# The feed-forward up projection by Strassen's scheme, with f kept in DRAM until the down projection

## What is computed

```python
def conv_ffn(h, w_up, conv_w, conv_b, w_down):      # h: 1024 x 1024, D_FF = 2816
    s = h.shape[1]
    u = h @ w_up                                     # 1024 x 5632
    u_pad = jnp.pad(u, ((0, 0), (CONV_WIDTH_2 - 1, 0), (0, 0)))
    u = conv_b + conv_w[0] * u_pad[:, 0:s] + conv_w[1] * u_pad[:, 1:1 + s] + conv_w[2] * u_pad[:, 2:2 + s]
    gate = u[..., :D_FF]
    val = u[..., D_FF:]
    return (jax.nn.silu(gate) * val) @ w_down        # back to 1024 x 1024, added to x
```

## Time and profile before

| | us |
|---|---|
| median of 3 runs | 2482.22 (2477.52 to 2484.29) |
| profiled execution, its own time | 2483.62 |
| its span | 2482.0 |
| PE busy | 2451.3 (99%) |
| DVE busy | 1416.7 (57%) |
| ACT busy | 806.5 (32%) |
| POOL busy | 95.5 (4%) |

### The profile page before, as it was taken

How to read it: one execution, slowest core, us unless ns; L and a number is a source line. 1 busy time by engine, 2 the same in 40 slices (tenths; PEclk the granted TensorE clock), 3 DMA queues, 4 the chain that set the end, 5 groups by cost and what they waited for, 6 DMA issues and landing times.

```text
span 2482.0 us, 31910 instructions
## 1 busy us (share of the span) xinstructions
PE 2451.3 (99%) x11696; PEld 2036.9 (82%) x11696; DVE 1416.7 (57%) x2288; ACT 806.5 (32%) x1513; POOL 95.5 (4%) x112
## 2 busy tenths in 40 slices
PE   8999999999999999999999999999999999999998
PEld 6888888888888888887788888988888888888876
DVE  5747887787532243436455753553687257734775
ACT  5334544444521121321233352453232112211224
POOL 1000000000000000021000020012000000000000
PEclk9999999999999999999999999999999999999999
DMA  5111111111111131222110142451111111111123
GB/s 197 34 43 52 43 51 51 43 59 46 48 51 51 46 115 51 86 75 56 35 46 26 35 140 85 137 178 51 43 51 48 45 51 51 44 50 51 44 63 123
DMA packets 236403, 160.97 MB, mean 65 GB/s; under 512 B 5294, under 2 KB 223571, under 8 KB 235298
## 3 DMA queue, kind: packets, MB, share of 16 engines
q1 hardware_dynamic: 229456, 132.66, 18.0%
q0 software_dynamic: 4976, 18.75, 2.2%
q10 hardware_dynamic: 1890, 8.43, 1.0%
HBM read 138.85 MB, written 20.97 MB: 64 GB/s over the span
## 4 chain that ended last, share of the span: by engine, by line
PE 96%; DVE 2%; DMA 1%; ACT 1%; issue 0%; SPq 0%; ACTq 0%; DVEq 0%
PE bank L717 26%; PE bank L718 26%; PE bank L719 26%; PE bank L1051 1%; PE bank L872 1%; PE bank L1052 1%; PE bank L1053 1%; PE bank L1248 1%; PE bank L1250 1%; PE bank L1249 1%; PE bank L1104 1%; PE bank L1103 1%; PE bank L1105 1%; DMA wraw<-in_w_in_dram 1%; PE bank L883 1%; PE bank L884 1%
## 5 line engine op out<-in xcount | busy, mean ns | idle before, releaser
L717 PE MATMUL bank<-xhi,whi 128*128 128x512 f32 x1056 | 411.8, 390 | 0.6 <-DVE wlo L1860 0.6
L719 PE MATMUL bank<-xhi,wlo 128*128 128x512 f32 x1056 | 410.9, 389 | 0.0
L718 PE MATMUL bank<-xlo,whi 128*128 128x512 f32 x1056 | 410.9, 389 | 0.0
L1860 DVE TENSOR_TENSOR wlo<-wraw,whi 128x1024 fp32r<-128x1024 f32 (+1 forms) x240 | 285.3, 1189 | 151.4 <-ACT whi L1282 101.6
L1289 ACT ACTIVATE whi<-wraw 128x1024 fp32r<-128x1024 f32 x132 | 139.5, 1057 | 573.9 <-PE bank L719 569.1
L717 PE MATMUL bank<-x4hi,whi 128*128 128x512 f32 x704 | 274.3, 390 | 0.0
L719 PE MATMUL bank<-x4hi,wlo 128*128 128x512 f32 x704 | 273.9, 389 | 0.0
L718 PE MATMUL bank<-x4lo,whi 128*128 128x512 f32 x704 | 273.9, 389 | 0.0
L717 PEld LDWEIGHTS bank<-xhi,whi 128*128 128x128 f32 x1056 | 198.2, 188 | 42.5 <-DVE wlo L1860 0.7
L718 PEld LDWEIGHTS bank<-xlo,whi 128*128 128x128 f32 x1056 | 198.2, 188 | 41.5 <-issue 0.2
L719 PEld LDWEIGHTS bank<-xhi,wlo 128*128 128x128 f32 x1056 | 198.2, 188 | 41.3
(11 more groups left out here) (397 smaller groups left out, 4515.2 us busy)
## 6 DMA issues: line engine op xcount, KB each, us to landing
wraw<-in_w_in_dram SPq DMA_DIRECT2D x85, 512.0 KB, 3.9
wraw<-in_ffn_w_up_dram SPq DMA_DIRECT2D x44, 512.0 KB, 3.8
wraw<-in_xattn_wkv_dram SPq DMA_DIRECT2D x16, 512.0 KB, 4.0
wraw<-in_ffn_w_down_dram SPq DMA_DIRECT2D x16, 512.0 KB, 4.0
wraw<-in_ffn_w_down_dram SPq DMA_DIRECT2D x16, 384.0 KB, 3.5
xraw<-in_x_dram SPq DMA_DIRECT2D x4, 1024.0 KB, 10.1
x_spill<-xt SPq DMA_DIRECT2D x8, 512.0 KB, 2.8
conv_spill<-tv POOLq DMA_DIRECT2D x8, 512.0 KB, 3.1
```

Source lines behind the costliest of these rows:

```text
L717: pe.matmul(acc, whi[slot][:, k, :], xh, start=(k == 0), stop=False)
L718: pe.matmul(acc, whi[slot][:, k, :], xl, start=False, stop=False)
L719: last = pe.matmul(acc, wlo[slot][:, k, :], xh, start=False, stop=(k == k_tiles - 1))
L1860: dve.tensor_tensor(wlo[slot][:, 0:n, :], wraw[slot][:, 0:n, :], whi[slot][:, 0:n, :].bitcast(F32), ALU.subtract).then_inc(s_wlo, 1)
```

## The change

The 1024 x 1024 block of x and the 1024 x 256 block of weights of a pair are each seen as 2 by 2 blocks: the two halves of the tokens and the two halves of the 8 feature blocks for x, the same halves of the feature blocks and gate against value for the weights. Strassen's scheme in Winograd's form gives the four result blocks (gate and value for each half of the tokens) by seven products of half the depth instead of eight.

- The seven right-hand forms of x (`b11`, `b21`, `b22` as they are, `t1` to `t4` sums and differences) are made once, the first four behind the attention's output projection, the others during the first pair, by DVE (`form_sum`, `form_lo`) and ACT (`form_hi`). They take the place of `x4hi` and `x4lo`.
- The seven left-hand forms of each pair's weights (`a11`, `a12`, `a22`, `s1` to `s4`) are made for every pair: POOL makes the four sums (`weight_sum`), ACT seven high parts (`weight_hi`), DVE seven low parts (`weight_lo`), each of 128x512.
- PE's `form_product` is 4 blocks times 3 matmuls. Products 2, 3, 5 and 6 (counted from 0) add onto a bank that holds an earlier product, which must first have been copied out (`first_copy` on ACT) or added (`result` on DVE).
- The factor `R` is now multiplied in by POOL for three of the four quarters (`normed`), by DVE for one. ACT computes the first tap (`tap0`), DVE the other two (`taps`), POOL the product of silu and value (`product`).
- f is not split at once: `store_f` writes it to DRAM. The down projection comes after all 22 pairs; `load_f` brings f back, ACT and DVE split it (`f_hi`, `f_lo`, 128x1024 each), and three accumulations over 8, 8 and 6 blocks follow.

The diff, cut to its core:

```diff
+PRODUCTS = (("a11", "b11"), ("s2", "t2"), ("a12", "b21"), ("s3", "t3"), ("s1", "t1"), ("a22", "t4"), ("s4", "b22"))
...
+            def form_product(n, p, ready=None):
+                a, b = PRODUCTS[n]
+                o, onto = ps(FORM_BANKS[n]), n in (2, 3, 5, 6)
+                pe.wait_ge(s_alo, 7 * p + (lo_order.index(a) + 1))
+                for k in range(HK):
...
+                    pe.matmul(o, ahi[a][:, k, :], xh, start=(k == 0 and not onto), stop=False, skip_group_check=True)
+                    pe.matmul(o, ahi[a][:, k, :], xl, start=False, stop=False, skip_group_check=True)
+                    last = pe.matmul(o, alo[a][:, k, :], xh, start=False, stop=(k == HK - 1), skip_group_check=True)
+                last.then_inc(s_m, 1)
...
+                pe.wait_ge(s_p1, p + 1)
+                form_product(2, p, (lambda k: 3 * k + 5) if first else None)
...
+            def weight_sum(name, p):                    # GpSimd
+                if name == "s3":
+                    ins = pool.tensor_tensor(to, a11, a21, ALU.subtract)
+                if name == "s2":
+                    ins = pool.tensor_tensor(to, a22, araw["s3"][:, :, :], ALU.subtract)
+                if name == "s1":
+                    ins = pool.tensor_tensor(to, a21, a22, ALU.add)
+                if name == "s4":
+                    ins = pool.tensor_tensor(to, a12, araw["s2"][:, :, :], ALU.subtract)
...
+            def normed(p, u, h, n):
+                pool.wait_ge(s_c, 6 * p + n)
+                pool.tensor_tensor(u_h, u_h, R[:, h * HALF:(h + 1) * HALF], ALU.mult).then_inc(s_rm, 1)
+            def product(p, h):
+                pool.wait_ge(s_act, 2 * p + h + 1)
+                pool.wait_ge(s_tap, 4 * p + 2 + h)
+                pool.tensor_tensor(yv[:, half], yv[:, half], yg[:, half], ALU.mult).then_inc(s_prod, 1)
...
+            def first_copy(p):                          # ScalarE
+                act.wait_ge(s_m, 7 * p + 1)
+                    act.wait_ge(s_tap, 4 * p - 1)
+                act.activation(uv[:, 2:2 + HALF], ps(2 * G0), ACT.Copy).then_inc(s_p1, 1)
...
+            def weight_lo(name, p):                     # VectorE
+                if name in ("s2", "s3"):
+                    dve.wait_ge(s_as, 4 * p + (4 if name == "s2" else 2))
+                dve.tensor_tensor(alo[name][:, :, :], src, ahi[name][:, :, :].bitcast(F32), ALU.subtract)\
+                    .then_inc(s_alo, 1)
...
+            def f_lo(n):
+                dve.wait_ge(s_ffn_hi, n + 1)
+                dve.tensor_tensor(flo[n][:, :], fraw[n][:, :], fhi[n][:, :].bitcast(F32), ALU.subtract)\
+                    .then_inc(s_ffn_lo, 1)
```

More of the change, by code:

```diff
@@ L63 @@
 T_FF = T_XO + 8
-T_LAST = T_FF + sum(2 * n + 8 for n in FF_GROUPS) - 8
+T_LAST = T_FF + 16
 T_END = T_LAST + 16
@@ L318, in hybrid_then_mixer_kernel @@
         s_par2 = sem("later_params_loaded")
+        s_part = [sem(f"part_loaded{n}") for n in range(8)]
         s_x = [sem(f"x_loaded{n}") for n in range(4)]
@@ L1714, in _ @@
             x_q_hi(0, 0)
[L1715 removed]
+            act.wait_ge(s_pw_loaded, 32)
             for a in range(2):
@@ new lines, in _ @@
+            act.wait_ge(s_ms, 8)
+            act.activation(x4root[:, :], ps(6)[:, 0:NB], ACT.Sqrt, bias=eps[:, 0:1], scale=1.0 / D).then_inc(s_rs, 2)
+            late_hi(5)
+            form_term(7)
+            late_hi(6)
+            late_hi(7)
+            for h in range(2):
+                act.wait_ge(s_ms, 9 + h)
+                act.activation(R[:, h * HALF:(h + 1) * HALF], ps(6 + h), ACT.Copy).then_inc(s_r, 1)
+            for k in range(HK):
+                form_hi("b22", k, resid[:, HK + k, HALF:S], gain(HK + k))
@@ new lines, in _ @@
+            up_step(0, first=True)
+            with act.Fori(1, LASTP) as i:
+                up_step(i)
+            up_step(LASTP, last=True)
+            tap0(LASTP, uv, yv, 1, 3, FF_TILES)
+            f_hi(5)
+            tap0(LASTP, ug, yg, 1, 4, 0)
+            f_hi(6)
+            tanh(LASTP, 1)
+            f_hi(7)
+            act.wait_ge(s_m, 7 * FF_TILES)
+            for n in range(8, 12):
+                load_f(n)
+            for n in range(8):
+                split(T_FF + n + 2, (T_FF + n) % 2)
+                f_hi(8 + n)
+                if n == 0:
+                    act.wait_ge(s_fst, 16 * FF_TILES)
+                if n < 4:
+                    load_f(12 + n)
@@ new lines, in _ @@
+            late_lo(4)
+            late_sum(6)
+            late_lo(5)
+            result(2, 0)
+            late_sum(7)
+            late_lo(6)
+            late_lo(7)
+            weight_lo("a22", 0)
+            result(3, 0)
+            for k in range(HK):
+                form_lo(25 + k, "b22", k, HK + k, 1)
+            weight_lo("s4", 0)
+            result(4, 0)
+            dve.wait_ge(s_r, 8)
+            result(1, 0)
+            weight_lo("a11", 1)
+            weight_lo("a12", 1)
@@ new lines, in _ @@
+            taps(0, ug, yg, 0, 1, 0)
+            silu(0, 0)
+            weight_lo("s3", 1)
+            weight_lo("s2", 1)
+            weight_lo("s1", 1)
+            weight_lo("a22", 1)
+            with dve.Fori(1, LASTP) as i:
+                order.enter(i, 4, 1)
+                up_step(i)
+                order.leave(LASTP)
+            up_step(LASTP, last=True)
+            result(5, LASTP)
+            f_lo(4)
+            taps(LASTP, uv, yv, 0, 2, FF_TILES)
+            taps(LASTP, uv, yv, 1, 3, FF_TILES)
@@ new lines, in _ @@
+            f_lo(5)
+            taps(LASTP, ug, yg, 1, 4, 0)
+            f_lo(6)
+            silu(LASTP, 1)
+            f_lo(7)
+            for n in range(16):
+                t = T_FF + n
+                for h in range(2):
+                    dve.wait_ge(s_acc, 2 * t + h + 1)
+                    r = resid[:, n % KT, h * HALF:(h + 1) * HALF]
+                    dve.tensor_tensor(r, ps(2 * (t % 2) + h), r, ALU.add).then_inc(s_free, 1)
+                split(t + 2, t % 2)
+                if 8 + n < FF_TILES:
+                    f_lo(8 + n)
```

665 lines of the change are left out of this document (516 added, 149 removed).

## The result

The changed kernel takes 2554.97 us (median of 4 runs, 2551.22 to 2557.13), the kernel before 2482.41 (4 runs, 2477.52 to 2484.29): a ratio of 1.0289, with a 95% interval from 1.0276 to 1.0302. The forecast was 2554, in a range from 2478 to 2620. The mechanism was right.

What follows compares the result with a forecast made beforehand. PE was taken as the bound. First pair 20.0, second 7.5, others 20 x 1.6, squares -1.9, down tile 11.0, clock 3: 71 us on 2483.6 gave 2555, median 1.4 lower, so 2554; range 2478 to 2620.

Steps and rivals of the forecast that it cites:

- The bound before: In the feed-forward network PE alone is the bound: two waits, 1.3 us out of 718 us.
- the matmuls taken away: In the 22 pairs, 264 matmuls fewer, 59.9 us; 84 remain per pair, 19.05 us.
- The exclusion: In the pairs, POOL operations reading SBUF and DVE operations with two SBUF inputs exclude one another; together 22.1 us per pair.
- Rival one: No exclusion counts in the loop, PE bounds it at 19.05 us per pair: -26 us, 2456 us; chance 0.18.
- The fixed part read from the copies: Some 0.18 us of a POOL operation do not scale with columns, so one of 128x512 takes 1.29 us.
- The chain in the loop: From the end of product 5 to product 2, 12.2 us; PE waits 4 us, a pair takes 23.35.
- three operations of POOL come first (3.8 us): After product 5, value times R, the s4 sum and value times R precede DVE's low parts: 3.8 us.
- small waits: In each loop pair, short PE waits before products 5 and 6, about 0.3 us.
- The clock: Rival: the clock falls in every pair behind the product 2 wait, 2.7 us x 21 = 57 us, 2611; chance 0.13.
- The ends: First pair 41.8 us instead of 21.8, plus 3 for clock; second 29.2; PE waits 11.0 in the first down tile.
- the sums over squares: Behind the attention, two sums over squares now lie within the first pair: 1.9 us taken off.
- The rows to look for: Profile after: 84 matmuls in 23 to 24 us, longest PE wait at product 2, POOL operations 1.3 to 1.9, PE share 88%.

Runs made afterwards that it cites:

- section 2: Changed kernel with POOL's two-SBUF-input operations in the feed-forward part replaced by a tiny operation and eight memsets, so almost no reads: 2451.18 us, ratio 0.987.
- sections 1, 2 and 5: Section 1 and section 2 have their own lines; 5 is the changed kernel with DVE's second and third taps summing in PSUM: 2475.69 us.
- The own tile: Changed kernel with ACT's copy of product 0 put in a tile of its own: 2522.66 us.
- the other orders: Changed kernel with the own tile, copy and result 0 earlier in ACT's and DVE's queues, POOL's first sums ahead of the last sum of squares, no PSUM: 2524.01 us.
- the two moves on POOL: Changed kernel with gate-value products behind all taps, 2505.49 us; separately, with the fourth weight sum ahead of the second value half times R, 2510.46 us.
- the PSUM operands: Changed kernel with ACT's first tap written to PSUM and DVE's second and third taps using the running sum there: 2475.69 us, ratio 0.9968.
- the dose run: Changed kernel with only POOL's four weight sums per pair replaced by a tiny operation and eight memsets: 2489.8 us, a single run.
- the fastest kernel: Changed kernel with the other orders, taps through PSUM, and POOL's fourth weight sum moved ahead of value times R: 2460.95 us, 0.9921 of the kernel before.
- section 1: Separate kernel of only 128x512 operations, each engine alone, then two together: 16 on DVE beside 8 on POOL take 18.24 us, against 19.5 one after the other.

## Why the prediction was right, and where it was not

**The bound before and the matmuls taken away** were right: section 2 shows 19.04 us per pair where no read of POOL interferes.

**The exclusion** was right, including the inference that DVE is held when POOL is first; sections 1, 2 and 5 show it. Rival one, no exclusion in the loop, forecast 2456 us. That is near what the run without reads gives (2451, though that run leaves work of POOL out), with the loop at 19.04 us as the rival had it: its premise was false, and its sum stood up. The fixed part read from the copies gave 1.29 us for a POOL operation of 128x512; weight sums and unheld products show 1.29, the operations with R 1.09.

**The chain in the loop** was mis-sized: from the end of product 5 to product 2 I walked 12.2 us, and the trace has 10.95 (product 6 starts at 1997.03, product 2 at 2007.98). The step that failed is "three operations of POOL come first (3.8 us)". They take 3.4 (1996.99 to 2000.38), because two of the three are the 1.09 us form. The rest of the walk takes 7.6 us instead of 8.4, since low parts and taps overlap their hand-overs more than I allowed. The pause was thus 2.64 us, not 4, and small waits 0.5, not 0.3.

**The clock** was put into a rival with 0.13, on the ground that the pause might be too short or that products 0 and 1 stand before it. In fact it fell in every pair, at a pause even shorter than I assumed, and cost 1.71 us rather than 2.7. As terms of the loop, 19 pairs at +1.6 were 30 us and measured +2.12 each, 40.3. So the step that failed here is the term for the clock, put at nothing in the sum. Per pair the pause was 4.0 - 2.64 = 1.36 too much, the clock and the small waits 1.71 + 0.19 too little; 0.54 are left, 23.89 against 23.35. That they nearly cancel is luck.

**The ends** were over-priced. The first pair takes 39.3 us with its clock loss (forecast 41.8 + 3). Product 0 waits 1.58 us, not 3.2. Product 1 waits 7.71, not 8.8, and then takes 5.21 us, mostly at 1.2 GHz (2.5 us lost, 3 expected). From product 3 on 6.3 us are added, not 7.9. And the 41.8 themselves don't add up: 19.05, the waits of 3.2, 8.8 and 7.9 and the 1.9 of the sums over squares are 40.85, so 0.95 us have no term. The second pair is 27.75, not 29.2, and 2.4 of that are clock which the forecast did not have (its product 1 takes 5.1 us). The first down tile takes 20.68 us, 9.8 more than its 10.88 (forecast 11.0 of waits); 6.0 are waits, and most of the rest is low clock behind the longest of them (granted 0.50 and 0.51 in the 8 us from 2294). Together: 17.5 + 6.0 + 40.3 + 1.65 (last pair) - 1.9 + 9.8 = 73.35 us, against 20 + 3 + 7.5 + 30.4 + 1.6 - 1.9 + 11 = 71.6. The ends gave back 8 of the 10 us that the loop lacked, and nothing in the working made sure of that.

**The rows to look for** came as said, apart from two: PE's longest total wait at product 2 behind ACT's `ffn_u_value` (51.2 us), 84 matmuls in 23.89 us, DVE's taps up to 1.63, PSUM operations at 0.68. POOL's operations lie between 1.09 and 1.70, not 1.3 and 1.9. PE's share, too, was not as said: it was 96% of the span and 90% of the loop, not 88%, because a slow matmul counts as busy; the granted clock of 0.93 in the loop was the row to watch.

What stays open: how the 3.13 us of pauses divide between held time and order. The own tile, alone and with the other orders (22.11 and 22.20), shows that they move without shrinking; the two moves on POOL take 0.8 of them each; the PSUM operands take 2.3. These shares overlap, since a shorter hold also moves the next.

## To carry to other kernels

Before work goes to an idle GpSimd, list which of its operations and of VectorE's read SBUF, and add both lists as if they were one engine's; if the sum nears the bound engine's time, give VectorE's operations a PSUM operand where a bank is free, and order GpSimd's queue so that what others wait for isn't behind what waits itself. A pause of TensorE in a loop has two prices, its length and the low clock behind it: splitting or filling it can pay as much as removing it. The longest wait in the profile names one dependency, not the bound, and freeing it alone can move the wait.

## What the hardware showed that I had not expected

- Operations with one SBUF operand take part in the exclusion: DVE's tensor_scalar and POOL's copy (section 1). In the run without reads POOL's additions of 4 columns are shown with 0.2 to 0.66 us on average, by tile. A small read waits behind a long one as well: the one shown first below lasts until 1975.01, and DVE's tap beside it until 1974.96; where DVE is not in the way such an addition takes 0.20 us.

```profile
1974.38 0.63 POOL L777 TENSOR_TENSOR ffn_u_gate<-ident 128x4 f32<-128x4 f32 x1 [1.59 <-DVE ffn_u_gate L3068]
...
1974.22 0.74 DVE L3075 SCALAR_TENSOR_TENSOR ffn_value<-ffn_u_value,pcol,ffn_value 128x512 f32<-128x512 f32 x1
...
L777 POOL TENSOR_TENSOR ffn_u_gate<-ident 128x4 f32<-128x4 f32 x21 | 13.8, 658 | 32.7 <-DVE ffn_u_gate L3068 32.7
```

- PE's clock is sensitive to small differences of a pause that recurs: behind 2.48 us of waiting it was granted 0.57 in the next 4 us, behind 1.76, 1.61, 1.53 and 1.16 us (orders without PSUM, the two moves on POOL and the dose run) 1.00. A change that shortens the pause from the one to the other gains 1.7 us on top. The length of the wait alone doesn't decide: in the fastest kernel the clock was 1.00 in the 4 us behind a wait of 2.66 us in its second pair, and 0.61 behind one of 1.85 us in its last. What else decides no run here shows.

```profile
1782.89 0.50 PE L1382 MATMUL bank<-t_hi,s_hi 128*128 128x512 f32 x1 [2.66 <-DVE s_lo L2957]
1783.00:1787.00 4.00, 4.00 (x18) 3.31 (x19) 3.72 (x6) 2.64 (x5) 1.70 (x2) 1.00 0.78 227
...
2183.74 0.50 PE L1382 MATMUL bank<-t_hi,a_hi 128*128 128x512 f32 x1 [1.85 <-DVE ffn_u_value L3057]
...
2184.00:2188.00 4.00, 4.00 (x12) 3.13 (x12) 3.40 (x4) 4.00 (x5) 1.36 (x1) 0.61 0.38 98
```

- A running sum in PSUM costs a tap nothing: 745 to 753 ns with the operand there, 752 in SBUF.
